# Two output projections of a one-core transformer block moved from plain fp32 matmuls to three passes over high and low parts

## The reference, cut to what matters

```python
merged = sigmoid(z_g) * (o_g @ w_proj_gla) + sigmoid(z_m) * (o_m @ w_proj_moba)    # first block
x = x + merged @ w_out
merged = g_diff * (o_diff @ w_o_diff) + g_sb * (o_sb @ w_o_sb)                     # each layer
x = x + merged @ w_out
```

## Time and profile before

| | before |
|---|---|
| median of runs | 1678.44 us |
| profiled execution | 1674.33 us |
| its span | 1672.3 us |
| PE busy | 1454.1 us (87%) |
| DVE busy | 737.2 us (44%) |
| ACT busy | 548.9 us (33%) |

### The profile page before, as it was taken

The page is one execution under the profiler, slowest core; times in us unless marked ns, Lnnn a source line. Parts: engine busy times, 40 slices in busy tenths (PEclk is TensorE's granted clock), DMA queues, the critical chain, the costliest instruction groups (busy, mean ns, idle before and its releaser), DMA issues.

```text
span 1672.3 us, 22984 instructions
## 1 busy us (share of the span) xinstructions
PE 1454.1 (87%) x10155; PEld 1178.7 (70%) x10155; DVE 737.2 (44%) x1074; ACT 548.9 (33%) x671; POOL 2.9 (0%) x8
## 2 busy tenths in 40 slices
PE   7998999878676576666799999999999999999998
PEld 6696888643223232232489888999988988899997
DVE  2555724331011010110487655666456675666643
ACT  2462422311001010010334843443343573454431
POOL 0000000000000000000000000000000000000000
PEclk9997999979889888898899999999999999999999
DMA  6642129449999999999445315556452421655640
GB/s 218 214 166 101 53 100 370 172 189 420 422 420 422 421 421 421 420 422 421 160 155 177 122 51 201 164 190 219 177 184 101 152 101 51 219 183 166 214 152 26
DMA packets 129803, 374.50 MB, mean 224 GB/s; under 512 B 9271, under 2 KB 54631, under 8 KB 105127
## 3 DMA queue, kind: packets, MB, share of 16 engines
q1 hardware_dynamic: 125735, 370.71, 58.1%
q0 software_dynamic: 528, 2.04, 0.4%
q10 hardware_dynamic: 3440, 0.25, 0.2%
HBM read 371.92 MB, written 1.06 MB: 223 GB/s over the span
## 4 chain that ended last, share of the span: by engine, by line
PE 65%; DMA 14%; DVE 9%; SPq 6%; ACT 4%; issue 1%; ACTq 1%; DVEq 0%
PE bank L588 32%; DMA ring<-in_w_exp_up 8%; PE bank L1096 7%; SPq L476 5%; DMA SZ<-in_w_exp_up 5%; PE bank L612 4%; PE bank L930 3%; DVE parts L1531 3%; PE bank L806 3%; PE bank L909 2%; PE bank L953 2%; PE bank L566 2%; PE bank L634 2%; DMA ring<-in_w_out 1%; ACT parts L1193 1%
## 5 line engine op out<-in xcount | busy, mean ns | idle before, releaser
L588 PE MATMUL bank<-hnr,parts 128*128 128x256 f32 x4032 | 496.6, 285 | 0.0
L588 PEld LDWEIGHTS bank<-hnr,parts 128*128 128x128 f32 x4032 | 489.6, 193 | 5.1 <-issue 4.8
L1531 DVE TENSOR_TENSOR parts<-ring,parts 128x2048 fp32r<-128x2048 f32 x136 | 306.2, 2287 | 129.8 <-ACT parts L1193 129.4
L1193 ACT ACTIVATE parts<-ring 128x2048 fp32r<-128x2048 f32 x136 | 252.8, 1902 | 164.1 <-DMA ring<-in_w_out 59.1
L930 PE MATMUL bank<-ring,G 128*32 128x512 f32 x768 | 114.7, 752 | 91.1 <-DMA ring<-in_w_exp_up 90.4
L1861 DVE COPY SQ<-bank 64x512 f32<-64x512 f32 x16 | 16.8, 1049 | 314.5 <-PE bank L930 314.5
L930 PEld LDWEIGHTS bank<-ring,G 128*32 128x32 f32 x768 | 30.0, 133 | 174.3 <-issue 105.9
L588 PE MATMUL bank<-SKr,parts 128*128 128x256 f32 x960 | 123.0, 290 | 11.7 <-DVE SKr L1697 9.7
L588 PEld LDWEIGHTS bank<-SKr,parts 128*128 128x128 f32 x960 | 120.3, 198 | 14.8 <-issue 9.2
L1096 PE MATMUL bank<-Gr,parts 128*128 128x256 f32 x640 | 115.3, 283 | 0.0
L1326 ACT ACTIVATE SQ<-bank 64x512 f32<-64x512 f32 x16 | 16.8, 1050 | 268.6 <-PE bank L930 268.6
(11 more groups left out here) (300 smaller groups left out, 1388.1 us busy)
## 6 DMA issues: line engine op xcount, KB each, us to landing
ring<-in_w_in SPq DMA_DIRECT2D x60, 1024.0 KB, 7.3
ring<-in_w_exp_gate SPq DMA_DIRECT2D x48, 1024.0 KB, 26.3
ring<-in_w_exp_up SPq DMA_DIRECT2D x48, 1024.0 KB, 26.9
ring<-in_w_exp_down SPq DMA_DIRECT2D x48, 1024.0 KB, 26.3
ring<-in_w_ffn_in SPq DMA_DIRECT2D x44, 1024.0 KB, 7.7
ring<-in_w_ffn_out SPq DMA_DIRECT2D x20, 1024.0 KB, 6.0
hx<-in_w_exp_gate SPq DMA_DIRECT2D x16, 1024.0 KB, 26.0
SZ<-in_w_exp_up SPq DMA_DIRECT2D x16, 1024.0 KB, 27.0
```

Source lines behind the costliest of these rows:

```text
L588: m = mm(b(name)[:, T * half:T * half + T], part(chunk, ws)[:, k, P * mt:P * mt + P], src[xs][:, k, :], start=k == 0 and i == 0, stop=k == ...
L1193: A(parts[:, 2 * (r % 2), 2048 * i:2048 * i + 2048], ring[:, CHUNK[chunk][0], 2048 * i:2048 * i + 2048], ACT.Copy).then_inc(high_made, 1)
L1531: v.tensor_tensor(parts[:, 2 * (r % 2) + 1, at], ring[:, CHUNK[chunk][0], at], parts[:, 2 * (r % 2), at].bitcast(F32), ALU.subtract).then_ ...
```

## The change

`proj_*` chunks join `SPLIT` (two more per stage, so every other chunk keeps its half of `parts`). The activations of the first attention are split in two pieces each by ACT (`first_highs`) and DVE (`first_lows`); the copies of `mo*` and `bo*` out of PSUM are replaced by a high copy on ACT (`second_highs`) and a subtraction on DVE (`second_lows`), which is what frees the bank now. In the layers the head norms move from h = 4 to 7 to h = 1, 3 and 5 (two).

```diff
-SPLIT = [n for n in ALL_CHUNKS if not n.startswith(("ckv", "proj", "cq", "co"))]
+SPLIT = [n for n in ALL_CHUNKS if not n.startswith(("ckv", "cq", "co"))]
...
+            def merge_out(sfx, chunks, second, n):
+                for chunk, src, names in ((chunks[0] + sfx, first_parts, "pa"), (chunks[1] + sfx, second_parts, "pb")):
+                    for j in range(4):
+                        name = f"{names}{j}{sfx}"
+                        room(pe, name)
                         for half in range(2):
+                            mt = 2 * j + half
                             for k in range(4):
+                                ready(chunk, k, 4)
+                                if mt == 0 and names == "pa" and k % 2 == 0:
+                                    pe.wait_ge(first_split, 2 * n + k // 2 + 1)
+                                if mt == 0 and names == "pb":
+                                    emptied(pe, f"{second}{k}{sfx}")
+                                for i, (ws, xs) in enumerate(PASSES):
+                                    m = mm(..., part(chunk, ws)[:, k, P * mt:P * mt + P], src[xs][:, k, :], ...)
...
# ACT, both stages
+            def first_highs(n, o):
+                act.wait_ge(og_ready, n + 1)
+                for i in range(2):
+                    A(two(first_parts[0], i), two(o, i), ACT.Copy).then_inc(first_high, 1)
+            def second_highs(name, i):
+                full(act, name)
+                A(second_parts[0][:, i, :], b(name)[:, 0:T], ACT.Copy).then_inc(second_high, 1)
# ACT, first block, loop over h = 2..7
+                if h % 2 == 0:
+                    second_highs(f"mo{h // 2 - 1}", h // 2 - 1)
                 take_turned(f"mt_{h}", h)
...
                 take((...)[h - 2], ...)
...
+                if h >= 6:
+                    high("proj_gla", [h - 6])
+                if h == 6:
+                    first_highs(0, og)
...
-            sigmoids(["zg3", "zm3"])
+            second_highs("mo3", 3)
+            sigmoid("zg3", z1)
+            high("proj_moba")
+            sigmoid("zm3", z2)
# ACT, layers, end of the loop over h
+                    if h in (2, 4, 6):
+                        second_highs(f"bo{h // 2 - 1}{x}", h // 2 - 1)
+                    if h in (5, 6):
+                        high("proj_diff" + x, [h - 5])
+                    if h == 6:
+                        first_highs(l + 1, od)
# DVE, first block
             for h in range(2, 8):
                 moba_norm(h)
                 if h % 2 == 0:
-                    (copy of mo{h // 2 - 1})
+                    second_lows(f"mo{h // 2 - 1}", 0, h // 2 - 1)
...
                 if h < 6:
                     low("zm0" if h < 4 else "zm1", [h % 2])
+                else:
+                    low("proj_gla", [h - 6])
+                if h == 6:
+                    first_lows(0, og)
+            second_lows("mo3", 0, 3)
# DVE, merge
+                        if names == "pb" and j == 0:
+                            low("out0" + x, [0])
                         (pa/pb times gate)
+                        if names == "pa" and j < 2:
+                            low(("proj_sb" if x else "proj_moba") + x, [j])
...
+                            if j == 0:
+                                low("out0" + x, [1])
                             if j == 1:
-                                low("out0" + x)
                                 z_low(n, 0)
# DVE, layers
-                    if h >= 4:
-                        last = head_apply(od, ["dn0" + x, "dn1" + x], h - 4, subs)
-                    if h == 7:
+                    for i in {1: (0,), 3: (1,), 5: (2, 3)}.get(h, ()):
+                        last = head_apply(od, ["dn0" + x, "dn1" + x], i, subs)
+                    if h == 5:
                         last.then_inc(og_ready, 1)
                     if h in (2, 3):
                         low("gb1" + x, [h - 2])
-                    if h % 2 == 1:
-                        (copy of bo{h // 2})
+                    if h in (2, 4, 6):
+                        second_lows(f"bo{h // 2 - 1}{x}", l + 1, h // 2 - 1)
+                    if h == 7:
+                        first_lows(l + 1, od)
+                    if h >= 6:
+                        low("proj_diff" + x, [h - 6])
+                second_lows("bo3" + x, l + 1, 3)
```

More of the change, by code:

```diff
@@ L810, in merge_out @@
                 split_f("out1" + sfx, z_parts, ["ou2" + sfx, "ou3" + sfx])
-            merge_out("", ["proj_gla", "proj_moba"], og, lambda: pe.wait_ge(og_ready, 1),
-                      om, lambda: [emptied(pe, f"mo{i}") for i in range(4)], 0)
+            merge_out("", ["proj_gla", "proj_moba"], "mo", 0)
             norm_sum("n_cross")
@@ L1078, in _ @@
                     sb_out(h)
-                merge_out(x, ["proj_diff" + x, "proj_sb" + x], od, lambda: pe.wait_ge(og_ready, l + 2),
-                          ob, lambda: [emptied(pe, f"bo{i}{x}") for i in range(4)], l + 1)
+                merge_out(x, ["proj_diff", "proj_sb"], "bo", l + 1)
                 norm_sum("n_ffn" + x)
@@ L1278, in _, with sigmoid @@
                     high("zm1", [h - 3])
[L1280 to L1283, removed]
-            sigmoids(["zg3", "zm3"])
+                if h >= 6:
+                    high("proj_gla", [h - 6])
+                if h == 6:
+                    first_highs(0, og)
+            def sigmoid(name, z):
+                emptied(act, name)
+                A(z, z, ACT.Sigmoid).then_inc(z_sig, 1)
+            second_highs("mo3", 3)
+            sigmoid("zg3", z1)
+            high("proj_moba")
+            sigmoid("zm3", z2)
             high("out0")
@@ L1443, in _ @@
                         high("gb1" + x, [h - 2])
-                sigmoids(["ga3" + x, "gb3" + x])
+                    if h in (2, 4, 6):
[4 more added lines that the diff above has]
+                        first_highs(l + 1, od)
+                sigmoid("ga3" + x, z1)
+                second_highs("bo3" + x, 3)
+                high("proj_sb" + x)
+                sigmoid("gb3" + x, z2)
                 high("out0" + x)
@@ L1663, in head_apply, with first_lows, second_lows @@
                 return v.scalar_tensor_tensor(o[:, h, :], o[:, h, :], col, hroot[:, h, :], ALU.mult, ALU.mult)
+            def first_lows(n, o):
+                for i in range(2):
+                    dve.wait_ge(first_high, 2 * n + i + 1)
+                    v.tensor_tensor(two(first_parts[1], i), two(o, i), two(first_parts[0], i).bitcast(F32), ALU.subtract).then_inc(first_split, 1)
+            def second_lows(name, n, i):
+                dve.wait_ge(second_high, 4 * n + i + 1)
+                freed(v.tensor_tensor(second_parts[1][:, i, :], b(name)[:, 0:T], second_parts[0][:, i, :].bitcast(F32), ALU.subtract), name)
             head_squares(og)
```

26 lines of the change are left out of this document (8 added, 18 removed).

## The result

The changed kernel takes 1689.05 us (median of 5 runs, 1686.22 to 1690.77) against 1679.49 us for the kernel before in the same measurement (5 runs, 1674.84 to 1681.9): ratio 1.0055, 95% interval 1.0037 to 1.0073, so 9.6 us slower. The forecast was 1682.4 us with a range of 1671 to 1690. The profiled execution took 1689.05 us, its span 1687.2.

The account below looks back on a forecast made before the run. PE bounds the kernel, busy 87% of the span. First block +6.0, layer 0 -0.35, layer 1 -1.7, together +3.9 us: 1678.3 us profiled, 1682.4 us on the median, range 1671 to 1690.

Parts of the forecast that it names:

- What the change removes: Merges: projections 4.6 us shorter each, `out0`/`out1` 3.1, 4.6 and 4.5 us shorter; -26.0 us if nothing else moved.
- First block: First block's sum: 3.25 us without clock plus 2.7 us of clock, +6.0 us.
- Late subtractions: First block, even heads: `second_highs` delays the chain, PE loses 0.85 us at h = 3 and h = 5: +1.7 us.
- Idle at `mt_7`: First block, h = 6: `moba_norm(7)` queues behind `proj_gla`'s low half and `first_lows`; PE idle 5.95 us.
- six matmuls into `pa`: First block, h = 7: PE waits for the second half of `proj_gla`, idle 3.3 us.
- clock: First block: one drop of 1.5 us for the 5.95 us idle, 0.8 for the 3.3 us: +2.7 us.
- Layers, the bank: Layers: `bo0`'s bank freed late, `ba4` idle 6.6 us, `gb2` 1.5 us; each layer -2.6 (-2.5 in layer 1) without clock.
- rival 2: Clock falls at every new idle, six at 2.0 us each: +4.8 us, so 1687.2 us; chance 0.20.
- The expert stage between passes a shift on: Expert stage: its fetches are released by PE's own progress, so it passes on a shift; no size of its own.
- The offset: Whole kernel: profiled execution lies 4.1 us below the 1678.44 us median, so 1678.3 gives 1682.4 us on the median.
- Rival 1: Layers: `bo0`'s late release does not hold PE, each layer about -7.3 us; total -8.6, 1669.8 us; chance 0.16.
- Rival 3: Merges: `out0` starts no earlier, the 12.2 us stay unspent: 1694.6 us; chance 0.06.

Follow-up runs that it names:

- all reorderings and padding: Changed kernel with banks swapped, norms, `proj_*` parts and high halves reordered, plus 120 no-wait instructions in PE's expert stage: 1648.38 us, ratio 0.9848.
- repeated kernel before: The kernel before, unchanged, run again for a second profile: 1677.96 us, ratio 0.9999.
- The moving wait: Changed kernel with the layers' four head norms at turns 3, 4, 5, 5 instead of 1, 3, 5, 5: 1685.48 us, ratio 1.0045.
- both edits: Changed kernel with `moba_norm(7)` ahead of `proj_gla`'s low half and `ba4`/`bz6`, `gb2`/`ba7` swapped in the bank plan: 1663.24 us, ratio 0.992.

## Why the prediction was right, and where it was short

**What the change removes: right.** Projections 23.29 us where 23.3 was said; the gap in `out0` 0.92 us where about 1.0 was said; end of `pb` to end of `out1` 24.2 us where 24.3 was said. I put it at 26.0 us if nothing else moved. In the kernel with all reorderings and padding, next to nothing else moves, and A, C and D lie 8.7, 8.9 and 8.2 us under those of the repeated kernel before: 25.8 us.

**First block: right.** Late subtractions cost 0.65 us a time (8.70 us from `mt_2` to `mt_3`, 8.05 before), where I took 0.85 within 0 to 1.2. Idle at `mt_7` 5.88 us for 5.95, six matmuls into `pa` 3.11 for 3.3, clock 1.34 + 1.75 = 3.1 for 2.7. A rose by 5.9 us (5.0 against the repeat) for the 6.0 of the sum. The edit that moves the norm showed the cause: queue order on DVE alone.

**Layers, the bank: right in place and idle, short in clock.** `ba4` stood 6.63 us for 6.6, `gb2` 1.24 for 1.5, ended by the subtraction that replaces the copy; the swap of banks, in which no DVE instruction moves, took both bank waits away. The step that was mis-sized is "I count ... one for the idle before `ba4` in each layer and half a one at `gb2`: +2.25". Both fell, in both layers. In layer 0 it cost 1.22 - 0.70 + 4.72 - 3.12 = 2.1 us at `ba4` and 4.59 - 3.12 = 1.5 at `gb2`: 3.6 us, and in layer 1, in the same way, 3.3. C came to +1.1 and D to -0.6 where I had -0.35 and -1.7: 2.5 us. Here rival 2 came true, at 1.4 to 2.1 us a fall instead of 2.0.

**The step that failed** is "The expert stage between passes a shift on, since its fetches are released by PE's own progress." Its weights do (389 to 391 us from the end of the first to the end of the last long wait, in all profiles), but behind the branch PE stood 3.6 to 3.7 us that I had at nothing. It hangs on the length of PE's program, which I never counted.

**The offset.** I carried the 4.1 us between the profiled execution and the median over to the forecast. B varies by 5.8 us between two profiles of the kernel before, and the first has the short one, so that fits. Together, 1682.4 + 2.5 + 3.7 = 1688.6 us against 1689.05 measured. That the time lies in the range is owed to its width: it is 0.95 us under the top, rival 2's 1687.2 is nearer than my 1682.4, and I had the change at less than half of the 9.6 us that it costs. The agreement of the mended sum is partly luck as well, since it takes single profiled executions, and against the repeat C and D rose by 0.3 and 0.6 us and not by 1.1 and -0.6.

**The other rivals.** Rival 1 (bank wait harmless) fell at once. Rival 3 (`out0` no earlier) fell by the 24.2 us. The moving wait shows why thinning out DVE's turns ahead of `bo0` is no remedy: the second bank is behind the same queue.

**Open.** What makes the clock fall at a given idle in one execution and not in the next, and whether the changed kernel's runs (none under 1686.2 of eleven) favour a long B, or just came so. Where the boundary behind the stand lies.

## What to carry to other kernels

When a copy out of PSUM is replaced by something later in its engine's queue, look up which group has that bank next and when it wants it: here two late releases cost 16.6 us, and handing other banks to two groups, without moving any work, gave them back. A faster pass pays only once what feeds it stands in the queues in the order in which TensorE will ask. And read the stretches that were not touched as well: a longer program can move a taken branch to a place where it costs some 3 to 4 us, and a trial with padding tells that from everything else.

## What the runs showed of the hardware that I had not expected

- A taken branch of TensorE cost nothing (up to 0.2 us) or let it stand 2.7 to 4.1 us, by where the code stands; the branch instruction itself took 0.91 to 1.00 us or 3.3 to 4.9. Padding of 112 to 128 instructions switched it on or off.
- Equal idles had unequal effect on the granted clock: 2.08 us ahead of `ba4` of layer 0 dropped it with the banks swapped and did not with both edits; 2.37 and 2.36 us ahead of `ba6` in one execution left it up once and dropped it once. An idle of 1.24 us, some 19 us behind one of 6.63, dropped it in both layers, while the one of 0.92 us ahead of `out0` never did.
- A stretch with the same instructions (from `out1` to the first wait for expert weights) took 120.6 or 125.6 us in two profiles of one kernel, for the most part by the clock; a difference of 5 us between medians is not yet the effect of an edit.
